# Gate and up of a conv-FFN with the weights as the stationary operand

## The reference, cut to what matters

```python
def conv_gated_ffn(x, w_up, conv_w, conv_b, w_down):
    gu = x @ w_up                                  # 2048 -> 2 x 5632
    gate, up = gu[..., :D_FF], gu[..., D_FF:]
    gate = causal_depthwise_conv(gate, conv_w, conv_b)   # CONV_W = 3
    return (jax.nn.silu(gate) * up) @ w_down

for i in range(DEPTH):                             # 2
    u = rms_norm(h, norm_mix_g[i]) @ w_in[i]
    ...                                            # pooling mixer, latent attention
    h = h + jnp.concatenate([y_pool, y_att], axis=-1) @ w_out[i]
    h = h + conv_gated_ffn(rms_norm(h, norm_ffn_g[i]), w_up[i], conv_w[i], conv_b[i], w_down[i])
    gate = jax.nn.sigmoid(rms_norm(h, norm_ple_g[i]) @ w_ple_gate[i])
    h = h + (p[i] @ w_ple[i]) * gate
return rms_norm(h, final_norm_g)
```

## Time and profile before

| | us |
|---|---|
| median of 3 runs | 2231.83 (2231.7 to 2231.89) |
| the profiled execution | 2233.44 |
| its span | 2231.8 |
| PE busy in the span | 2203.0 |
| DVE busy | 1383.2 |
| ACT busy | 1053.6 |

### The profile page before, as it was taken

The page is one execution under the profiler, slowest core; times in us unless marked ns, Lnnn a source line. Parts: engine busy times, 40 slices in busy tenths (PEclk is TensorE's granted clock), DMA queues, the critical chain, the costliest instruction groups (busy, mean ns, idle before and its releaser), DMA issues.

```text
span 2231.8 us, 31546 instructions
## 1 busy us (share of the span) xinstructions
PE 2203.0 (99%) x10594; PEld 1855.2 (83%) x10594; DVE 1383.2 (62%) x1770; ACT 1053.6 (47%) x1368; POOL 47.3 (2%) x138
## 2 busy tenths in 40 slices
PE   8999999999999999999999999999999999999997
PEld 7898888888888888888898988888888888888885
DVE  6567566656666656676556665566656566656655
ACT  6545444444444444445464554444444444444554
POOL 4000000000000000000010000000000000000000
PEclk9999999999999999999999999999999999999998
DMA  7644555555655555645555356555555555555562
GB/s 240 208 152 151 180 185 188 182 194 169 207 188 188 177 199 169 207 170 197 178 184 171 131 174 201 177 189 187 188 187 173 203 189 188 188 182 173 190 208 75
DMA packets 233886, 406.60 MB, mean 182 GB/s; under 512 B 14969, under 2 KB 50249, under 8 KB 233673
## 3 DMA queue, kind: packets, MB, share of 16 engines
q1 hardware_dynamic: 232177, 401.81, 53.8%
q10 hardware_dynamic: 1256, 2.15, 0.3%
q0 software_dynamic: 368, 1.58, 0.2%
HBM read 403.42 MB, written 2.10 MB: 182 GB/s over the span
## 4 chain that ended last, share of the span: by engine, by line
PE 98%; ACT 0%; DVE 0%; DMA 0%; issue 0%; SPq 0%; ACTq 0%; POOLq 0%; DVEq 0%; POOL 0%
PE acc L1427 31%; PE acc L1429 31%; PE acc L1428 31%; PE tps L1484 3%; PE tps L1428 1%; PE tps L1429 0%; PE tps L1427 0%; DMA raw<-in_w_in 0%; PE tps L1679 0%; DVE h L1410 0%; DVE w_lo L1023 0%; ACT sq_h L656 0%; ACT w_hi L615 0%; ACT up_tok L863 0%; PE tps L1574 0%
## 5 line engine op out<-in xcount | busy, mean ns | idle before, releaser
L1023 DVE TENSOR_TENSOR w_lo<-raw,w_hi 128x1024 fp32r<-128x1024 f32 (+1 forms) x772 | 914.5, 1214 | 506.8 <-ACT w_hi L844 352.1
L844 ACT ACTIVATE w_hi<-raw 128x1024 fp32r<-128x1024 f32 x508 | 525.9, 1059 | 499.9 <-PE acc L1429 499.9
L1427 PE MATMUL acc<-w_hi,xa_hi 128*128 128x512 f32 (+1 forms) x1792 | 690.4, 385 | 0.8 <-DVE xa_lo L1034 0.8
L1429 PE MATMUL acc<-w_lo,xa_hi 128*128 128x512 f32 (+1 forms) x1792 | 686.8, 383 | 0.0
L1428 PE MATMUL acc<-w_hi,xa_lo 128*128 128x512 f32 (+1 forms) x1792 | 686.0, 383 | 0.0
L1429 PEld LDWEIGHTS acc<-w_lo,xa_hi 128*128 128x128 f32 x1792 | 336.9, 188 | 65.8
L1427 PEld LDWEIGHTS acc<-w_hi,xa_hi 128*128 128x128 f32 x1792 | 337.2, 188 | 65.2 <-issue 1.6
L1428 PEld LDWEIGHTS acc<-w_hi,xa_lo 128*128 128x128 f32 x1792 | 337.2, 188 | 63.7
L615 ACT ACTIVATE w_hi<-raw 128x1024 fp32r<-128x1024 f32 (+1 forms) x264 | 266.5, 1044 | 161.5 <-PE acc L1429 151.2
L1427 PE MATMUL acc<-w_hi,gt_hi 128*128 128x512 f32 x640 | 250.7, 392 | 0.0
L1429 PE MATMUL acc<-w_lo,gt_hi 128*128 128x512 f32 x640 | 249.1, 389 | 0.0
(11 more groups left out here) (196 smaller groups left out, 1352.6 us busy)
## 6 DMA issues: line engine op xcount, KB each, us to landing
raw<-in_w_up SPq DMA_DIRECT2D x176, 1024.0 KB, 5.0
raw<-in_w_down SPq DMA_DIRECT2D x88, 1024.0 KB, 4.9
raw<-in_w_out SPq DMA_DIRECT2D x32, 1024.0 KB, 5.0
raw<-in_w_ple_gate SPq DMA_DIRECT2D x32, 1024.0 KB, 5.0
raw<-in_w_in SPq DMA_DIRECT2D x22, 1024.0 KB, 5.3
raw<-in_w_ukv SPq DMA_DIRECT2D x8, 1024.0 KB, 5.2
raw<-in_w_in SPq DMA_DIRECT2D x8, 864.0 KB, 4.9
raw<-in_w_uq SPq DMA_DIRECT2D x6, 1024.0 KB, 6.0
```

Source lines behind the costliest of these rows:

```text
L844: copy(w_hi[:, half_of(m), :], raw[:, c % RAW_SLOTS, (m % 2) * HALF:(m % 2 + 1) * HALF], ACT.Copy).then_inc(hi_done, 1)
L1023: dve.tensor_tensor(w_lo[:, half_of(m), 0:n], raw[:, c % RAW_SLOTS, at:at + n], w_hi[:, half_of(m), 0:n].bitcast(F32), ALU.subtract).then_ ...
L1427: pe.matmul(dst, a_hi, b_hi, start=first, stop=False)
L1429: return pe.matmul(dst, a_hi, b_lo, start=False, stop=last)
```

## The change

Gate and up make the weights the stationary operand: each half has four tiles of 128 output features, and for each tile and each of its two k tiles `three` streams the 256 tokens of `xa` into one half of a bank. Gate's four tiles go to the four banks of both `acc` pairs, up's to the four banks of `tps`. The results have features on partitions, so `rows_out`, `gate_tok`, `up_tok` and `turn_rows` go. The factor of a token now lies along the free dimension: once a layer, in unit 0, DVE spreads `rstd` over columns (`rows_spread`), TensorE transposes two tiles of it (job "rows") and DVE keeps it as `rstd_row` (`rows_kept`). DVE multiplies gate by it on the way out of `acc`, convolves out of SBUF, multiplies the silu by it (`by_row`), and multiplies by up straight out of `tps`. `down` 0 and 1 use `acc`, `down` 2 and 3 use `tps`. `xa` is one tensor with hi and lo side by side. Counts of blocks and jobs follow (`ACC_UNIT`, `JOB_UNIT`), and `turned` gives the count of `t_ready`.

```diff
@@ -48,6 +48,10 @@
 BLK = 512
 LATE = (6, 6, 4)
 T_BANKS = 4
+ACC_UNIT = 4
+JOB_UNIT = 8
+ROWS_JOBS = 5
+P_JOBS = 4
...
-        xa = (sb("xa_hi", [P, KT, S], F32R), sb("xa_lo", [P, KT, S], F32R))
+        x_both = sb("xa", [P, KT, 2, S], F32R)
+        xa = (x_both[:, :, 0, :], x_both[:, :, 1, :])
...
-            gate_tok = sb("gate_tok", [P, TT, BLK], scope=scope)
-            up_tok = sb("up_tok", [P, TT, BLK], scope=scope)
+            gate_f = sb("gate_f", [P, 4, S], scope=scope)
+            up_f = sb("up_f", [P, 4, S], scope=scope)
             conv = sb("conv", [P, 4, S], scope=scope)
-            sig = sb("sig", [P, 4, S], scope=scope)
+            rstd_row = sb("rstd_row", [P, S], scope=scope)
...
@@ -553,7 +579,7 @@
                 pool.wait_ge(sq_done, TT * (3 * N_BLK * l + SQ + N_BLK + 2))
                 factor(5 * l + 3, sumsq[:, :, :], rstd["ffn"], C_D, STEPS * l + 8)
 
-                pool.wait_ge(t_ready, JOBS * l + JB["ffn"] + 1)
+                block_ready(pool, l, BL["ffn"])
                 pool.dma_start(p_tok[:, :, :], p_v[bass.ds(l, 1)].rearrange("l p t n -> p (l t) n")).then_inc(
                     p_landed, 16)
...
-                    def at_block(k):
-                        block_ready(act, l, b0 + k, v)
-
-                    def rows_out(k, dst):
-                        at_block(k)
-                        for t in range(TT):
-                            copy(dst[:, t, :], acc[(b0 + k) % 2][:, t, :], ACT.Copy,
-                                 scale=rstd["ffn"][:, t:t + 1]).then_inc(acc_free[(b0 + k) % 2], 1)
-
                     if with_down:
                         go(0, 2)
-                        at_block(-1)
+                        halves_used(act, l, m0 - 1, v)
                         act.wait_ge(g_done, UNITS * l + u)
                         copy(gt[0][:, :, :], conv[:, :, :], ACT.Copy).then_inc(g_hi, 1)
-                    go(2, 8)
-                    if not with_down:
-                        act.wait_ge(rstd_done, 5 * l + 5)
-                    rows_out(0, gate_tok)
-                    go(8, 13)
+                    go(2, 13)
                     act.wait_ge(conv_done, UNITS * l + u + 1)
-                    copy(sig[:, :, :], conv[:, :, :], ACT.Tanh, scale=0.5).then_inc(tanh_done, 1)
-                    go(13, 16)
-                    rows_out(1, up_tok)
-                    if with_down:
-                        go(16, 24)
+                    copy(gate_f[:, :, :], conv[:, :, :], ACT.Tanh, scale=0.5).then_inc(tanh_done, 1)
+                    go(13, 24 if with_down else 16)
 
                 unit(l, 0, 0, False)
...
+                    def rows_spread():
+                        dve.wait_ge(rstd_done, 5 * l + 5)
+                        for t in range(TT):
+                            ins = dve.tensor_scalar(up_f[:, t, 0:P], ident[:, :], 0.0, rstd["ffn"][:, t:t + 1],
+                                                    ALU.mult, ALU.add)
+                        ins.then_inc(rows_wide, 1)
+
+                    def rows_kept():
+                        dve.wait_ge(t_ready, turned(l, JB["rows"]))
+                        dve.tensor_copy(rstd_row[:, :], tps[:, JB["rows"] % T_BANKS, 0:S]).then_inc(t_done, ROWS_JOBS)
+                        dve.wait_ge(t_done, JOBS * l + (JB["ffn"] + T_BANKS))
+                        dve.sem_inc(rows_done, 1)
+
+                    def by_row(x):
+                        return x, rstd_row[:, :].unsqueeze(1).broadcast_to([P, 4, S])
 
                     if with_down:
                         go(0, 2)
                         dve.wait_ge(g_hi, UNITS * l + u)
                         lo(gt[1][:, :, :], conv[:, :, :], gt[0][:, :, :]).then_inc(g_lo, 1)
-                    go(2, 11)
-
+                        go(2, 9)
+                    else:
+                        go(2, 4)
+                        rows_spread()
+                        go(4, 8)
+                        rows_kept()
+                        go(8, 9)
+                        dve.wait_ge(rows_done, l + 1)
+
+                    for k in range(2):
+                        block_ready(dve, l, b0 + k, vv)
+                        dve.tensor_tensor(gate_f[:, 2 * k:2 * k + 2, :], acc[k][:, :, 0:S],
+                                          rstd_row[:, :].unsqueeze(1).broadcast_to([P, 2, S]),
+                                          ALU.mult).then_inc(gate_step, 1)
+                        dve.wait_ge(gate_step, 2 * UNITS * l + 2 * u + (k + 1))
+                        dve.sem_inc(acc_free[k], 2)
+                    go(9, 10)
+                    go(10, 11)
                     for ft in range(4):
-                        if ft % 2 == 0:
-                            job_ready(ft // 2)
-                        dve.tensor_scalar(conv[:, ft, :], gate_t(ft), tap(2, ft),
+                        dve.tensor_scalar(conv[:, ft, :], gate_f[:, ft, :], tap(2, ft),
                                           prm[:, bass.ds(4 * u + (BIAS + ft), 1)], ALU.mult,
                                           ALU.add).then_inc(conv_step, 1)
+                    go(11, 12)
                     for ft in range(4):
                         dve.wait_ge(conv_step, c0 + (ft + 1))
-                        dve.scalar_tensor_tensor(conv[:, ft, 1:S], gate_t(ft)[:, 0:S - 1], tap(1, ft), conv[:, ft, 1:S],
+                        dve.scalar_tensor_tensor(conv[:, ft, 1:S], gate_f[:, ft, 0:S - 1], tap(1, ft), conv[:, ft, 1:S],
                                                  ALU.mult, ALU.add).then_inc(conv_step, 1)
+                    go(12, 13)
                     for ft in range(4):
                         dve.wait_ge(conv_step, c0 + (4 + ft + 1))
-                        ins = dve.scalar_tensor_tensor(conv[:, ft, 2:S], gate_t(ft)[:, 0:S - 2], tap(0, ft),
+                        ins = dve.scalar_tensor_tensor(conv[:, ft, 2:S], gate_f[:, ft, 0:S - 2], tap(0, ft),
                                                        conv[:, ft, 2:S], ALU.mult, ALU.add)
-                        if ft % 2:
-                            ins.then_inc(t_done, 1)
-                    dve.wait_ge(t_done, JOBS * l + 4 * vv + (j0 + 2 + T_BANKS))
-                    dve.sem_inc(conv_done, 1)
-                    go(11, 14)
+                    ins.then_inc(conv_done, 1)
+                    go(13, 15)
 
                     dve.wait_ge(tanh_done, UNITS * l + u + 1)
-                    dve.scalar_tensor_tensor(conv[:, :, :], sig[:, :, :], 1.0, conv[:, :, :], ALU.add,
+                    dve.scalar_tensor_tensor(conv[:, :, :], gate_f[:, :, :], 1.0, conv[:, :, :], ALU.add,
                                              ALU.mult).then_inc(silu_done, 1)
-                    go(14, 16)
+                    go(15, 16)
+                    dve.wait_ge(silu_done, 2 * UNITS * l + 2 * u + 1)
+                    dve.tensor_tensor(conv[:, :, :], *by_row(conv[:, :, :]), ALU.mult).then_inc(silu_done, 1)
 
                     def gated():
-                        dve.wait_ge(silu_done, UNITS * l + u + 1)
-                        for k in range(2):
-                            job_ready(2 + k)
-                            two = conv[:, 2 * k:2 * k + 2, :].rearrange("p a b -> p (a b)")
-                            dve.scalar_tensor_tensor(two, tps[:, (j0 + 2 + k) % T_BANKS, :], 0.5, two, ALU.mult,
-                                                     ALU.mult).then_inc(t_done, 1)
-                        dve.wait_ge(t_done, JOBS * l + 4 * vv + (j0 + 4 + T_BANKS))
-                        dve.sem_inc(g_done, 1)
+                        halves_used(dve, l, m0 + 15, vv)
+                        dve.wait_ge(silu_done, 2 * UNITS * l + 2 * u + 2)
+                        dve.scalar_tensor_tensor(conv[:, :, :], tps[:, :, 0:S], 0.5, conv[:, :, :], ALU.mult,
+                                                 ALU.mult).then_inc(g_done, 1)
+                        dve.wait_ge(g_done, UNITS * l + u + 1)
+                        dve.sem_inc(t_done, 4)
+
+                    def add_down(j):
+                        if j < 2:
+                            add_block(l, b0 + 2 + j, j, vv, False)
+                            return
+                        halves_used(dve, l, m0 + 17 + 2 * j, vv)
+                        for t in range(TT):
+                            hb = h[:, t, j * BLK:(j + 1) * BLK]
+                            dve.tensor_tensor(hb, tps[:, 2 * (j - 2) + t, :], hb, ALU.add).then_inc(t_done, 1)
 
                     if with_down:
-                        go(16, 19)
-                        add_block(l, b0 + 2, 0, vv, False)
+                        go(16, 17)
                         gated()
+                        go(17, 19)
+                        add_down(0)
                         go(19, 21)
-                        add_block(l, b0 + 3, 1, vv, False)
+                        add_down(1)
                         go(21, 23)
-                        add_block(l, b0 + 4, 2, vv, False)
+                        add_down(2)
```

(64 more changed lines are left out.)

62 lines of the change are left out of this document (38 added, 24 removed).

## The result

The changed kernel takes 2247.09 us in the median of four runs (2246.02 to 2247.84). The kernel before took 2231.76 us beside it. The ratio on record is 1.0066, with a 95% interval of 1.0054 to 1.0079: slower by 0.66%. The prediction said 2245.4 us, with 0.92 for slower. The profiled execution took 2247.65 us for a span of 2246.0 us, 14.2 us more than the span of before, at a mean granted clock of 0.997. The medians differ by 15.3 us and the profiled spans by 14.2. The 1.1 us between the two come from the choice of executions: the profiled one of before lay 1.7 us above the median of its runs, that of the changed kernel 0.6 above.

A forecast was written before the change was run, and what follows sets the result against it. TensorE's own instruction stream was taken as the bound: 20 loop units add 14.4 us, unit 0 in two layers takes off 0.8, so 2231.8 + 13.6 = 2245.4 us; own range 2240 to 2250, 8 in 10 from 2238 to 2258.

The forecast's parts named there:

- Products: Gate and up: 384 products of 256 columns at 0.1199 us replace 192 of 512 at 0.2268, +2.49 us a unit.
- Rival 2: Gate and up: 13 ns paid only where the bank changes, step near 0.1134 us, 2191 us in all; chance 0.04.
- Transposes: Sixteen transposes of gate and up a unit go, two groups at 0.887 us: -1.77 us a unit.
- Loop unit: Products and transposes net +0.72 us in each of 20 loop units, +14.4 us; units of 67.8 us.
- Unit 0: First unit of each of two layers: products, transposes, lost ScalarE wait, row factors and early need sum to -0.39 us.
- The need of acc[1]: Unit 0, gate's first half: TensorE waits some 0.2 us for VectorE's add out of acc[1]; bounds 0 and 1.5.
- The row factors: Unit 0: two added transposes for the row factors cost 0.29 us.
- Covers: VectorE at 44 of 67.8 us a unit: banks over 9 us to spare, splits 14 us less insertions of 3, cost 0.
- The margin at the end of the last unit: End of a layer's last unit, GpSimd's subtraction before TensorE: 0.56 us stays, cost 0; bounds 0 and 0.5 a layer.
- Rival 1: Longer unit body: instructions come too slowly, 2315 us, or are fetched at each jump back, 2317; chance 0.06.
- Rival 3: Gate and up: a step between, 0.1178 to 0.1188 us, time within 0.2% of before, 2227 to 2236; chance 0.03.
- Rival 4: Each unit: new wait of 0.2 to 1 us on acc, tps or a late split, 2249 to 2266 us; chance 0.10.

The follow-up runs named there:

- experiment 1: The changed kernel with gate and up's three products reordered to hi x hi, hi x lo, lo x hi, so two in a row share weights: span 2246.4 us.
- Experiment 2: The changed kernel with 16 transposes of the identity put back in every unit, their results overwritten: span 2282.6 us, +36.6.
- experiment 8: The changed kernel with ten more VectorE multiplies of 1024 elements a unit, behind gate's scaling: span 2277.0 us, +31.0.
- experiment 3: The changed kernel with gate and up streaming 192 of the 256 tokens, the last 64 columns left out: span 2174.3 us.
- experiment 7: The changed kernel with six more VectorE multiplies of 1024 elements a unit, behind gate's scaling: span 2244.2 us, unit 67.86 us as without them.
- experiment 9: The changed kernel with two products for three, grouped by 512 and 256 columns, group order turned every second half: 2213.05 us, 0.9915 of the kernel before.
- experiment 6: Against a two-product version of the changed kernel (span 2223.8 us), weights lo x x hi added into the bank's second half: span 2223.5 us.

## Why the prediction was right

*The bound.* TensorE, before and after: 98% of the chain. Its stream grew by 14.2 us, and so did the profiled span. Against the forecast of 13.6 us the loop units give 0.8 more (20 x 0.04) and the two units 0 give 0.26 less. The rest of the way from 2245.4 to the median of 2247.09 is scatter of single executions, which the mechanism does not explain.

*Products.* Forecast 0.1199 us a product from `by_feature`, measured 0.1200 in every pass of gate and up. The number on which everything hung came from a row with the same operands in the same engine at the same clock; that is why it fitted. Rival 2 (a step of 0.113, the fixed part paid only where the bank changes) falls with it: six products in a row into one half bank step by the same 0.12 as those across two. Its kin, paid where the stationary operand changes, falls with experiment 1. The sum needed only that the step at 256 columns is the one of `by_feature`; what in TensorE takes the 13 ns stays open.

*Transposes.* Forecast -1.77 us a unit. Experiment 2 puts them back at +1.73.

*Loop unit.* Forecast 67.82, measured 67.86.

*Unit 0.* Forecast -0.39, measured -0.52. The wait for `up_tok` is gone. The need of acc[1] costs 0.21 us where about 0.2 was forecast, on the half and the product that were named, but that the size fits is luck. The prediction let 0.13 us pass from the end of the add to TensorE's start; it was 0.05, the wait 0.10, and the other 0.10 is the longer step behind the restart, for which the prediction had no term. The row factors cost 0.14 + 0.08 = 0.22 us and not 0.29: the prediction took 0.099 for each transpose, an eighth of a group, while by the rows a first pair takes 0.14 and each further one 0.108.

*Covers.* VectorE is at 44.40 us a unit (forecast 44). For its splits the prediction had 14 us less an insertion of 3; experiment 8 measures 11.1 at the split of half 13. For the banks it had more than 9 us: `gated` ends at 434.52 and `down` 2 takes the tps banks at 443.99, 9.5 us later. The margin at the end of the last unit kept its 0.56 us.

*Rival 1,* instructions that come too slowly: 192 products in a row at 0.1200, ten units of 67.86 us one behind the other (319.15 + 10 x 67.86 = 997.75, where the next stage starts), no gap at the jump. The body of 480 pairs is fed as well as one of 304. In experiment 3 pairs pass at 0.112 us. Refuted. (The 0.105 us in which the prediction said that a pair can be issued is an average over eight transposes with a shorter last step; the rows give 0.108, which changes nothing here.) *Rival 3* falls with the step. *Rival 4:* no such row of waits, and experiment 7 shows that VectorE could have taken 7.5 us more in each unit for nothing.

*What the prediction did not see.* It took the fixed part of 13 ns for one that every product pays. It is not one at every length: at 192 columns a floor of 0.112 us has taken over. And it took the three products as given. The loss is in the form, not in the idea of keeping weights stationary: with two of the three products in one of 512 columns, and products of one length together, the same arrangement comes out 0.85% faster than before (experiment 9).

## What to carry to other kernels

Where the chain is one engine for 98% and its waits are a few microseconds, price a change by the step from start to start of the same instruction form elsewhere in the same trace, times the count; this gave the unit to 0.04 us. From 512 to 256 columns each product that is added costs about 13 ns. Here 192 of them a unit cost 2.53 us, and the transposes that they replaced had cost 1.77. So before weights are made stationary, weigh the products that are added against the work that goes, and see whether the moving side can still fill a bank, here by setting its hi and lo parts side by side. Put products of unlike length in groups of their own: in this kernel that was worth 9 to 12 us.

## What the hardware showed that was not expected

- In a steady stream a pair of weight load and product with 128 x 128 weights has a floor: 0.108 us a pair at 128 columns (transposes, experiment 2) and 0.1117 at 192 (experiment 3), then 0.1200 at 256, 0.1321 at 288 and 0.2266 at 512, the last three 12 to 13 ns above columns at 2.4 GHz.
- Products of 512 and 256 columns in turn cost 0.3528 us a pair, 6 ns more than their own steps. Grouped by eight a loop unit takes 66.41 us, and with groups of sixteen between the turns 66.29: about 0.03 us for a turn from 256 to 512, spread over the first five products of 512 columns behind it, of which about 0.01 comes back in the next group of 256. In strict alternation there is only one such product behind each turn, which fits the smaller 6 ns. What in the engine makes this stays open; the half of the bank that is written is not it (experiment 6).
- A wait that the view of waits gives as 1.25 us made the pass 1.49 us longer, because the step behind the restart is longer too, 0.22 for 0.12 (experiment 8; the same 0.22 in unit 0 of the changed kernel).
